# First mixers: scores of two neighbouring maps issued together, as products of 64 rows each

## The chip, the cores and the metric

One core of one Trainium2 chip runs the whole kernel. The metric is the device time of one execution in microseconds (us), taken as the median of several runs. A profiled execution beside them gives the trace that the rows below come from.

## What is computed

Two blocks of two layers each, on 256 tokens of width 1024, in float32. The first block is the one that matters here. Each of its two layers runs a feed-forward stage, a **mixer**, a second feed-forward stage and a gated embedding. The mixer is a windowed attention and a depthwise convolution side by side, gated and summed:

```python
u = rms_norm(h, norm_mix[i])
q, k, v, c, g = jnp.split(u @ w_in[i], splits, axis=-1)
q = rms_norm(q.reshape(B, S, N_HEADS, HEAD_DIM), q_norm[i])     # 8 heads of 64
k = rms_norm(k.reshape(B, S, KV_HEADS, HEAD_DIM), k_norm[i])    # 2 key heads of 64
y_attn = window_attention(q, k, v, sink[i], rel_bias) @ w_attn_out[i]
```

Four query heads share one key head. For every head the scores are 256 queries by 256 keys, each a sum over 64 products. The second block has mixers of its own (dilated, latent and differential attention), which the change leaves alone.

## The kernel before

**Matmuls and their weights.** Almost all the work is products of 256 rows with weights that stream in. The weights are cut into pieces (`ORDER`), mostly 1 MB. SyncE loads a piece into one of four `raw` slots; ScalarE rounds it to `whi` (line 1086, function `high`); VectorE forms the rest `wlo` (line 1608, function `low`); TensorE then makes three products for each of them (lines 498 to 500, 549 to 551, 576 and 582). ScalarE and VectorE prepare pieces that lie up to three ahead of the one TensorE works on (`AHEAD = 3`).

**Order of the work.** Every engine walks through the same program written out by hand. Side work, such as the attention of a mixer, is a Python generator on each engine, put into a list `bg`. A call of `tick()` advances every generator in the list by one step. TensorE ticks twice in a piece of four chunks (`rows`, lines 503 to 507), so that the attention's steps lie between runs of twelve products of 512 columns. VectorE ticks in `behind`: one tick, half of a piece of `wlo`, one tick, the other half. ScalarE ticks in `use`.

**The attention of a first mixer** (`attention1`, line 732 on TensorE, 1228 on ScalarE, 1849 on VectorE). Queries and keys are turned by products with the identity, so that the head dimension lies on the partitions. `qT` holds four pairs of query heads: in `qT[:, p, :]` the head that belongs to key head 0 lies on partitions 0 to 63 and the one of key head 1 on partitions 64 to 127. `kT` has two copies, `kT[:, s, :]`: copy s holds the keys of head s on its own 64 partitions, and zeros, written by VectorE (line 1910), on the other 64. The keys come out of the turn in one bank of PSUM, and ScalarE scales each half into its copy (line 1241). A product over all 128 partitions of `qT[:, p]` with `kT[:, s]` then gives the scores of one head.

There are eight maps (one per head), n = 0 to 7, pair p = n // 2 and key head s = n % 2. Step n of the generator does, on TensorE, `values1(n - 3)` (line 726), `turn1(n - 2)` (line 714) and `scores1(n)` (line 704). `scores1` makes two products, for queries 0 to 127 and 128 to 255, with 256 keys each. VectorE adds the bias and takes the row's extreme (line 1828), ScalarE takes the exponential (line 1218), and once TensorE has turned it (714), ScalarE copies it to `qn` (1226) as the stationary side of `values1`.

**Buffers for side work.** `spare()` (line 469) hands out three banks of PSUM in rotation, `P2` first half, `P2` second half, `SO` first half, and first waits for whatever frees the bank: for scores it is `s_mx` (VectorE has read both halves), for a turn it is `s_pTa` (ScalarE has copied it). The trace names these banks psP and psSO; the main products write psG.

**The same idea elsewhere in the kernel.** `scores2` (line 870), of the second block's mixers, handles maps of 32 and of 64 rows in pairs: it takes two banks, and issues for each half of the queries the product of the one map and then that of the other, on different partitions. Its first products have 128 columns (`SEGS`), the second ones 256. Maps of 96 rows are issued one at a time.

Of the kernel before, what the change touches and what calls it, by code (L numbers as in the profile page):

```python
# [8 lines left out]
F32 = mybir.dt.float32  # L9
F32R = mybir.dt.float32r  # L10
ACT = mybir.ActivationFunctionType
# [17 lines left out]
def piece(name, layer, chunks, *ranges):  # L29
    return (name, layer, tuple(chunks), tuple(ranges))  # L30
# [5 lines left out]
def halves(name, layer, *ranges, a=LO, b=HI):  # L36
    return [piece(name, layer, a, *ranges), piece(name, layer, b, *ranges)]
# [228 lines left out]
def build(nc, x_d, w_d, c_d, c2_d, rb_d, oh_d, msk_d, pt_d, line_d, out_d):  # L266
    with ExitStack() as ctx:
# [3 lines left out]
        def sem(name):  # L271
            return ctx.enter_context(nc.semaphore(name))
# [17 lines left out]
        def scope(n, names):  # L290
# [11 lines left out]
        M1 = scope(2, [  # L302
            ("y_hi", [128, 8, 256], F32R), ("y_lo", [128, 8, 256], F32R), ("thg", [128, 2, 2, 1024], F32),
            ("qs", [128, 2, 512], F32), ("qn", [128, 2, 512], F32), ("kv", [128, 2, 256], F32),
            ("qT", [128, 4, 256], F32), ("kT", [128, 2, 256], F32),
            ("acc", [128, 4, 256], F32), ("cpad", [128, 4 * 286], F32)])
        fill.close()
        c2 = sb("c2", [128, AT2["all"]])
# [10 lines left out]
        TB = (*BANKS["P2"], BANKS["SO"][0])  # L319
# [10 lines left out]
        s_xhi, s_xlo, s_tp, s_h, s_sq, s_ms, s_rs, s_half, s_dg, s_rsb, s_ones = (  # L330
            sem(n) for n in ("s_xhi", "s_xlo", "s_tp", "s_h", "s_sq", "s_ms", "s_rs", "s_half", "s_dg", "s_rsb", "s_ones"))
# [9 lines left out]
        s_lnc, s_nmu, s_lnq, s_lnv, s_lnr, s_ln, s_z, s_ychi, s_yclo = (  # L341
            sem(n) for n in ("s_lnc", "s_nmu", "s_lnq", "s_lnv", "s_lnr", "s_ln", "s_z", "s_ychi", "s_yclo"))

        s_qg, s_qs, s_qsq, s_qm, s_qr, s_qn, s_kv, s_km, s_kr, s_kn, s_kz, s_qT = (
            sem(n) for n in ("s_qg", "s_qs", "s_qsq", "s_qm", "s_qr", "s_qn", "s_kv", "s_km", "s_kr", "s_kn", "s_kz", "s_qT"))
        s_o, s_yhi, s_ylo, s_g, s_hm, s_cm, s_m = (sem(n) for n in ("s_o", "s_yhi", "s_ylo", "s_g", "s_hm", "s_cm", "s_m"))

        s_mx, s_ex, s_exs, s_pTa, s_pTv, s_pv = (
            sem(n) for n in ("s_mx", "s_ex", "s_exs", "s_pTa", "s_pTv", "s_pv"))
# [13 lines left out]
        def k(name, i=0, n=1):  # L363
            return cst[:, AT[name] + i:AT[name] + i + n]
# [7 lines left out]
        TBU = {}  # L372
# [7 lines left out]
        def flat(ap):  # L380
            return ap.rearrange("p a b -> p (a b)")
# [15 lines left out]
        thg, qs, qn, kv, qT, kT, acc = (M1[n] for n in ("thg", "qs", "qn", "kv", "qT", "kT", "acc"))  # L397
# [52 lines left out]
        def tensor(e):  # L450
# [18 lines left out]
            def spare(key):  # L469

                b = tb[1]
                TBU[key] = (tb[0], b)
                tb[0] += 1
                tb[1] = (b + 1) % 3
                f, i = spares[b]
                for s, v in f[i]:
                    e.wait_ge(s, v)
                return b

            def spare_frees(b, *when):  # L480
                f, i = spares[b]
                f[i] = list(when)
# [213 lines left out]
                free["SO"][1] = [(s_acc3, l + 1)]  # L696

            def scores1(l, n):
                p, s = n // 2, n % 2
                b = spare(("s1", l, n))  # L700
                e.wait_ge(s_qT, 4 * l + 4)
                e.wait_ge(s_kz, 2 * l + 2)
                for t in range(2):
                    i = e.matmul(TB[b][:, t * 256:t * 256 + 256], qT[:, p, t * 128:t * 128 + 128], kT[:, s, :], start=True, stop=True)
                i.then_inc(s_tp, 1)
                spare_frees(b, (s_mx, 2 * (8 * l + n) + 2))

            def turn1(l, n):
                b = spare(("p1", l, n))
# [8 lines left out]
            def values1(l, n):  # L718
                i4, s = n % 4, n % 2
                e.wait_ge(s_pTa, 8 * l + n + 1)  # L720
                for sm_, v in free["SO"][1]:
                    e.wait_ge(sm_, v)
                for t in range(2):
                    for kb_ in range(2):
                        c0 = kb_ * 256 + t * 128
                        i = e.matmul(O[:, t * 256 + i4 * 64:t * 256 + i4 * 64 + 64], qn[:, n % 2, c0:c0 + 128],
                                     kv[:, kb_, 128 + s * 64:192 + s * 64], start=kb_ == 0, stop=kb_ == 1)
                i.then_inc(s_pv, 1)
                if i4 == 3:
                    free["SO"][1] = [(s_o, 2 * (2 * l + n // 4) + 2)]  # L730

            def attention1(l):
                yield
                for n in range(2):
                    b = spare(("qT", l, n))
                    e.wait_ge(s_qn, 2 * l + 2)
                    for i in range(2):
                        for t in range(2):
                            ins = e.transpose(TB[b][:, i * 256 + t * 128:i * 256 + t * 128 + 128],
                                              qn[:, t, (2 * n + i) * 128:(2 * n + i) * 128 + 128], ident)  # L740
                    ins.then_inc(s_tp, 1)
                    spare_frees(b, (s_qT, 4 * l + n + 1))
                for _ in range(4):
                    yield
                b = spare(("kT", l))
                e.wait_ge(s_kn, 2 * l + 2)
                for t in range(2):
                    ins = e.transpose(TB[b][:, t * 128:t * 128 + 128], kv[:, t, 0:128], ident)
                ins.then_inc(s_tp, 1)
                spare_frees(b, (s_qT, 4 * l + 4))  # L750
                yield
                for n in range(11):
                    if n >= 3:
                        values1(l, n - 3)
                    if 2 <= n <= 9:
                        turn1(l, n - 2)
                    if n < 8:
                        scores1(l, n)
                    yield
                yield  # L760
                e.wait_ge(s_o, 4 * l + 4)
                for n in range(2):
                    transposes(("y", l, n), qs, (2 * n, 2 * n + 1), [(s_ylo, 2 * l + n + 1)])
# [294 lines left out]
        def scalar(e):  # L1058
# [169 lines left out]
            def attention1(l):  # L1228
                yield
                for n in range(2):  # L1230
                    u, b = TBU["qT", l, n]
                    e.wait_ge(s_tp, u + 1)
                    e.wait_ge(s_qg, l + 1)
                    e.activation(flat(qT[:, 2 * n:2 * n + 2, :]), TB[b][:, :], ACT.Copy, scale=sm[:, 0:1]).then_inc(s_qT, 1)
                for _ in range(4):
                    yield
                u, b = TBU["kT", l]
                e.wait_ge(s_tp, u + 1)
                for s in range(2):
                    r = slice(64 * s, 64 * s + 64)  # L1240
                    e.activation(kT[r, s, :], TB[b][r, 0:256], ACT.Copy, scale=k("k_norm", l)[r, :]).then_inc(s_qT, 1)
                yield
                for n in range(11):
                    if 2 <= n <= 9:
                        turn1(l, n - 2)
                    if n < 8:
                        softmax1(l, n)
                    yield
                yield
                for n in range(2):  # L1250
                    u, b = TBU["y", l, n]
                    e.wait_ge(s_tp, u + 1)
                    e.activation(flat(M1["y_hi"][:, 2 * n:2 * n + 2, :]), TB[b][:, :], ACT.Copy).then_inc(s_yhi, 1)
# [325 lines left out]
        def vector(e):  # L1579
# [236 lines left out]
            def scores1(l, n):  # L1816
                m = 8 * l + n
                hd = n // 2 + 4 * (n % 2)
                u, b = TBU["s1", l, n]
                for t in range(2):  # L1820
                    pb = tmp[:, (n % 4) * 512 + t * 256:(n % 4) * 512 + t * 256 + 256]
                    e.wait_ge(s_tp, u + 1)
                    if m == 0:
                        e.wait_ge(s_bias, 128)
                        e.wait_ge(s_dv, nsink_at)
                    if n >= 4:
                        e.wait_ge(s_tp, TBU["p1", l, n - 4][0] + 1)
                    e.tensor_tensor_reduce(pb, TB[b][:, t * 256:t * 256 + 256], bias[:, hd, 128 - 128 * t:384 - 128 * t], 1.0, nsink[:, 8 * l + hd:8 * l + hd + 1],
                                           ALU.add, ALU.min, sm[:, 64 + 2 * n + t:65 + 2 * n + t]).then_inc(s_mx, 1)
# [57 lines left out]
            def mixer1(l, nxt):  # L1887
# [17 lines left out]
                use(c0[0])  # L1905
                x_of_h("mix", l, 1)
                use(q[0])

                for s in range(2):
                    e.memset(kT[64 - 64 * s:128 - 64 * s, s, :], 0.0).then_inc(s_kz, 1)  # L1910
                e.memset(pad[:, :, 0:15], 0.0).then_inc(s_pad0, 1)
                e.memset(pad[:, :, 271:286], 0.0).then_inc(s_pad0, 1)
                e.tensor_scalar(sm[:, 0:1], k("q_norm", l), -0.125, None, ALU.mult, ALU.bypass).then_inc(s_qg, 1)
# [35 lines left out]
                for g in range(4):  # L1949
                    u = halves("w_in", l, (1792 + 512 * g, 2304 + 512 * g))  # L1950
# [36 lines left out]
                p, q = (piece("w_conv_out", l, LO, cols(g)) for g in range(2))  # L1987
# [8 lines left out]
                a, b = halves("w_o", l, cols(0)), halves("w_o", l, cols(1))  # L1996
# [530 lines left out]
```

## Time and profile before

| | |
|---|---|
| median of 3 runs | 1759.76 us (1759.19 to 1760.83) |
| the profiled execution's own time | 1759.31 us |
| its span, first to last instruction | 1757.5 us |
| TensorE busy | 1744.6 us, 99% of the span |
| VectorE busy | 1157.1 us, 66% |
| ScalarE busy | 930.6 us, 53% |
| read from memory | 300 MB, 171 GB/s over the span |

PE is TensorE's matmul and PEld its weight load, which overlaps it; DVE is VectorE, ACT ScalarE, POOL GpSimd, SP SyncE. Each float32 product with float32 operands shows as two MATMUL records, each with a LDWEIGHTS record of its own; the products with `whi` and `wlo` show as one. Matmuls are pipelined and their recorded ends are modelled, so durations of neighbours overlap; what a product costs is read from start to start.

### The profile page before, as it was taken

How to read it: one execution, taken by the hardware profiler on the slowest of the kernel's cores; microseconds unless marked ns; L12 is line 12 of the kernel's file. 1: busy time of each engine (PE TensorE's matmuls, PEld its weight loads, DVE VectorE, ACT ScalarE, POOL GpSimd, SP SyncE). 2: the span in 40 equal slices, each digit the busy share in tenths (PEclk: the TensorE clock that was granted, in tenths of full speed). 3: DMA queues.
4: the chain of work that ended last, by engine and by line, in shares of the span. 5: the costliest groups of instructions: out<-in, count | busy, mean ns of one | idle time of the engine just before them, and what ended most of it. 6: DMA issues, size and time to landing. Idle time of an engine off the chain costs nothing.

```text
span 1757.5 us, 26168 instructions
## 1 busy us (share of the span) xinstructions
PE 1744.6 (99%) x9886; PEld 1528.9 (87%) x9886; DVE 1157.1 (66%) x1700; ACT 930.6 (53%) x1376; POOL 26.5 (2%) x32
## 2 busy tenths in 40 slices
PE   9999999999999999999999999999999999999998
PEld 8888898898888988889889888889898888989886
DVE  6665588766655766568776665578575656857473
ACT  6554456655544555455655554467563546755352
POOL 0000000000000000000000000000000000000000
PEclk9999999999999999999999999999999999999999
DMA  8754523444545544552355445444265543435551
GB/s 314 219 192 169 214 102 139 175 176 183 192 170 190 210 183 173 190 198 101 128 190 189 183 173 192 163 157 163 99 213 192 192 165 112 152 120 194 202 181 48
DMA packets 45842, 303.04 MB, mean 172 GB/s; under 512 B 5104, under 2 KB 6256, under 8 KB 12312
## 3 DMA queue, kind: packets, MB, share of 16 engines
q1 hardware_dynamic: 45720, 301.36, 48.3%
q8 instruction: 83, 1.36, 0.3%
q14 instruction: 39, 0.32, 0.1%
HBM read 300.02 MB, written 1.31 MB: 171 GB/s over the span
## 4 chain that ended last, share of the span: by engine, by line
PE 97%; DVE 1%; ACT 1%; issue 1%; POOLq 0%; POOL 0%; ACTq 0%; DVEq 0%
PE psG L498 13%; PE psG L500 13%; PE psG L499 13%; PE psG L576 9%; PE psP L576 5%; PE psSO L576 5%; PE psG L582 5%; PE psG L549 3%; PE psG L550 3%; PE psG L551 3%; PE psSO L582 3%; PE psP L582 3%; PE psSO L693 2%; PE psP L615 1%; PE psSO L906 1%; PE psSO L500 1%
## 5 line engine op out<-in xcount | busy, mean ns | idle before, releaser
L1608 DVE TENSOR_TENSOR wlo<-raw,whi 128x1024 fp32r<-128x1024 f32 (+4 forms) x388 | 656.3, 1704 | 312.0 <-ACT whi L1086 311.8
L1086 ACT ACTIVATE whi<-raw 128x1024 fp32r<-128x1024 f32 (+4 forms) x388 | 554.1, 1444 | 276.3 <-PE psG L500 162.1
L498 PE MATMUL psG<-whi,x 128*128 128x512 f32 (+3 forms) x544 | 210.6, 387 | 0.0
L500 PE MATMUL psG<-whi,x 128*128 128x512 f32 (+3 forms) x544 | 200.9, 369 | 0.0
L499 PE MATMUL psG<-wlo,x 128*128 128x512 f32 (+3 forms) x544 | 200.5, 369 | 0.0
L498 PE MATMUL psG<-whi,hid_hi 128*128 128x512 f32 x472 | 184.1, 390 | 0.0
L500 PE MATMUL psG<-whi,hid_lo 128*128 128x512 f32 x472 | 183.6, 389 | 0.0
L499 PE MATMUL psG<-wlo,hid_hi 128*128 128x512 f32 x472 | 183.6, 389 | 0.0
L576 PE MATMUL psG<-x,whi 128*128 128x512 f32 x704 | 179.8, 392 | 0.0
L549 PE MATMUL psG<-x,wlo 128*128 128x256 f32 x512 | 147.5, 288 | 1.4 <-DVE wlo L1608 1.4
L576 PEld LDWEIGHTS psG<-x,whi 128*128 128x128 f32 x704 | 126.6, 189 | 22.6
L550 PE MATMUL psG<-x,whi 128*128 128x256 f32 x512 | 144.8, 283 | 0.0
L551 PE MATMUL psG<-x,whi 128*128 128x256 f32 x512 | 144.8, 283 | 0.0
L576 PE MATMUL psP<-x,whi 128*128 128x512 f32 x416 | 130.1, 394 | 0.0
L576 PE MATMUL psSO<-x,whi 128*128 128x512 f32 x416 | 128.9, 391 | 0.0
L498 PEld LDWEIGHTS psG<-whi,x 128*128 128x128 f32 x544 | 102.4, 188 | 16.1 <-issue 2.0
L500 PEld LDWEIGHTS psG<-whi,x 128*128 128x128 f32 x544 | 102.2, 188 | 15.6
L499 PEld LDWEIGHTS psG<-wlo,x 128*128 128x128 f32 x544 | 102.5, 188 | 14.1
L500 PEld LDWEIGHTS psG<-whi,hid_lo 128*128 128x128 f32 x472 | 88.6, 188 | 18.5
L499 PEld LDWEIGHTS psG<-wlo,hid_hi 128*128 128x128 f32 x472 | 88.6, 188 | 18.3
L498 PEld LDWEIGHTS psG<-whi,hid_hi 128*128 128x128 f32 x472 | 88.6, 188 | 18.1
L582 PEld LDWEIGHTS psG<-x,wlo 128*128 128x128 f32 x704 | 96.0, 190 | 6.8
(382 smaller groups left out, 2773.0 us busy)
## 6 DMA issues: line engine op xcount, KB each, us to landing
raw<-in_w SPq DMA_DIRECT2D x261, 1024.0 KB, 4.8
raw<-in_w SPq DMA_DIRECT2D x12, 768.0 KB, 4.2
raw<-in_w SPq DMA_DIRECT2D x14, 512.0 KB, 3.3
raw<-in_w SPq DMA_DIRECT2D x4, 576.0 KB, 3.8
raw<-in_w SPq DMA_DIRECT2D x4, 432.0 KB, 3.2
bias<-line_scratch SPq DMA_DIRECT2D x8, 192.0 KB, 10.3
h<-in_x SPq DMA_DIRECT2D x2, 512.0 KB, 5.9
out<-h SPq DMA_DIRECT2D x2, 512.0 KB, 2.7
```

Source lines behind the costliest of these rows:

```text
L498: e.matmul(o, ph, wh, start=first, stop=False)
L499: e.matmul(o, ph, wl, start=False, stop=False)
L500: i = e.matmul(o, pl, wh, start=False, stop=last)
L549: e.matmul(o, wl, x_hi[:, c, :], start=first and n == 0 and m % 2 == 0, stop=False)
L550: e.matmul(o, wh, x_lo[:, c, :], start=False, stop=False)
L551: i = e.matmul(o, wh, x_hi[:, c, :], start=False, stop=last and n == len(spec[2]) - 1 and m % 2 == 1)
L576: i = e.matmul(BANKS[bks[m // 2]][m % 2], wh, x[:, c, :], start=first and n == 0, stop=end)
L582: i = e.matmul(BANKS[bks[m // 2]][m % 2][:, 256:512], wl, x_hi[:, c, :], start=False, stop=False)
L615: ins = e.transpose(o, src[:, t, c * 128:c * 128 + 128], ident)
L693: e.matmul(O[:, 0:256], diag[:, tap % 16, :], pad[:, 1, tap:tap + 256], start=tap == 0, stop=tap == TAPS - 1).then_inc(s_cv, 1)
L1086: e.activation(w_at(whi, j, off, n), raw[:, j % RAW, off:off + n], ACT.Copy).then_inc(s_hi, count)
L1608: e.tensor_tensor(w_at(wlo, j, off, n), raw[:, j % RAW, off:off + n], f32(w_at(whi, j, off, n)), ALU.subtract).then_inc(s_lo, count)
```

## The change

The second copy of the keys goes: `kT` becomes 128 by 256, written by one ScalarE instruction over all partitions, and the zeros and their semaphore `s_kz` go. On TensorE, `scores1` does nothing for odd n; for even n it takes two banks and issues four products of 64 rows, in the order (queries 0 to 127: map n, map n + 1), (queries 128 to 255: map n, map n + 1). The last product of each map signals. VectorE waits, for either map, for the signal of the odd one.

```diff
-            ("qT", [128, 4, 256], F32), ("kT", [128, 2, 256], F32),
+            ("qT", [128, 4, 256], F32), ("kT", [128, 256], F32),
...
             def scores1(l, n):
-                p, s = n // 2, n % 2
-                b = spare(("s1", l, n))
-                e.wait_ge(s_qT, 4 * l + 4)
-                e.wait_ge(s_kz, 2 * l + 2)
-                for t in range(2):
-                    i = e.matmul(TB[b][:, t * 256:t * 256 + 256], qT[:, p, t * 128:t * 128 + 128], kT[:, s, :], start=True, stop=True)
-                i.then_inc(s_tp, 1)
-                spare_frees(b, (s_mx, 2 * (8 * l + n) + 2))
+
+                if n % 2:
+                    return
+                bs = [spare(("s1", l, n + s)) for s in range(2)]
+                e.wait_ge(s_qT, 3 * l + 3)
+                for t in range(2):
+                    for s, b in enumerate(bs):
+                        r = slice(64 * s, 64 * s + 64)
+                        i = e.matmul(TB[b][:, t * 256:t * 256 + 256], qT[r, n // 2, t * 128:t * 128 + 128], kT[r, :], start=True, stop=True)
+                        if t == 1:
+                            i.then_inc(s_tp, 1)
+                for s, b in enumerate(bs):
+                    spare_frees(b, (s_mx, 2 * (8 * l + n + s) + 2))
...
-                for s in range(2):
-                    r = slice(64 * s, 64 * s + 64)
-                    e.activation(kT[r, s, :], TB[b][r, 0:256], ACT.Copy, scale=k("k_norm", l)[r, :]).then_inc(s_qT, 1)
+                e.activation(kT[:, :], TB[b][:, 0:256], ACT.Copy, scale=k("k_norm", l)).then_inc(s_qT, 1)
...
             def scores1(l, n):
                 m = 8 * l + n
                 hd = n // 2 + 4 * (n % 2)
-                u, b = TBU["s1", l, n]
+                b = TBU["s1", l, n][1]
+
+                u = TBU["s1", l, n | 1][0]
...
-
-                for s in range(2):
-                    e.memset(kT[64 - 64 * s:128 - 64 * s, s, :], 0.0).then_inc(s_kz, 1)
```

The values that wait for `s_qT` change with it, from four signals a layer to three.

## Rows read from the trace of the kernel before

**Rows 1.** The page: busy time by engine, and TensorE's granted clock in 40 slices.

```profile
PE 1744.6 (99%) x9886; PEld 1528.9 (87%) x9886; DVE 1157.1 (66%) x1700; ACT 930.6 (53%) x1376; POOL 26.5 (2%) x32
...
PEclk9999999999999999999999999999999999999999
```

**Rows 2.** All waits of TensorE (six lines; first two, last): total us, times, longest.

```profile
PE psG L549 <- DVE wlo L1608: 1.4, 1, 1.4
PE psSO L1042 <- POOL ones L2369: 1.0, 1, 1.0
...
PE psSO L906 <- DVE mix L2096: 0.5, 2, 0.2
```

**Rows 3.** The tile kT: instructions that touch it, ns min/median/max, first and last start.

```profile
L704 PE MATMUL psP<-kT,qT x40: 377/379/382, 264.0 to 854.1; 128*128 128x256 f32 x40
...
L704 PE MATMUL psSO<-kT,qT x24: 377/379/382, 260.3 to 859.0; 128*128 128x256 f32 x24
L1910 DVE MEMSET kT<- x4: 272/272/272, 208.8 to 775.0; 64x256 f32 x4
L1241 ACT ACTIVATE kT<-psP,cst x4: 471/472/473, 257.8 to 824.2; 64x256 f32<-64x256 f32 x4
```

**Rows 4.** Timeline of TensorE, a step with scores, then one without (start, us, ...).

```profile
272.48 0.61 PE L714 MATMUL psP<-cst,tmp 128*128 128x128 f32 x4
...
274.02 0.40 PE L499 MATMUL psG<-wlo,x 128*128 128x512 f32 x1
...
296.88 0.61 PE L714 MATMUL psP<-cst,tmp 128*128 128x128 f32 x4
...
297.56 0.40 PE L499 MATMUL psG<-wlo,x 128*128 128x512 f32 x1
```

**Rows 5.** Timeline of TensorE, second block: a pair of 64-row maps, then no scores.

```profile
1233.01 0.50 PE L891 MATMUL psP<-cst,tmp 128*128 128x128 f32 x3
1233.44 0.37 PE L880 MATMUL psP<-qkcT,qkc 64*128 64x128 f32 x1
1233.45 0.37 PE L880 MATMUL psSO<-qkcT,qkc 64*128 64x128 f32 x1
1233.65 0.27 PE L880 MATMUL psP<-qkcT,qkc 64*128 64x128 f32 x1
...
1233.77 0.38 PE L880 MATMUL psP<-qkcT,qkc 64*128 64x256 f32 x1
...
1233.98 0.38 PE L880 MATMUL psP<-qkcT,qkc 64*128 64x256 f32 x1
...
1234.30 0.50 PE L498 MATMUL psG<-whi,c_hi 128*128 128x512 f32 x1
1234.63 0.39 PE L499 MATMUL psG<-wlo,c_hi 128*128 128x512 f32 x1
...
1236.39 0.50 PE L891 MATMUL psP<-cst,tmp 128*128 128x128 f32 x3
...
1236.96 0.39 PE L499 MATMUL psG<-wlo,c_hi 128*128 128x512 f32 x1
```

**Rows 6.** Timeline of VectorE in layer 0, around the first two maps.

```profile
261.40 0.48 DVE L1828 CUSTOM_DVE_ANT_0 tmp<-psSO,bias,sm 128x256 f32<-128x256 f32 x1
...
262.21 1.67 DVE L1788 SCALAR_TENSOR_TENSOR acc<-cpad,cst,acc 128x256 f32<-128x256 f32 x4
263.80 1.22 DVE L1608 TENSOR_TENSOR wlo<-raw,whi 128x1024 fp32r<-128x1024 f32 x1
265.03 0.48 DVE L1828 CUSTOM_DVE_ANT_0 tmp<-psP,bias,sm 128x256 f32<-128x256 f32 x1
```

**Rows 7.** Timeline of TensorE: the scores of maps 0 and 2.

```profile
260.34 1.02 PE L704 MATMUL psSO<-kT,qT 128*128 128x256 f32 x4
...
268.04 1.03 PE L704 MATMUL psSO<-kT,qT 128*128 128x256 f32 x4
```

**Rows 8.** Busy time by engine over the maps of layer 0.

```profile
258.00:296.00 38.00, 38.00 (x203) 32.79 (x203) 32.21 (x82) 26.02 (x62) 0.00 (x0) 1.00 0.32 112
```

More of the change, by code:

```diff
@@ L342, in build @@
             sem(n) for n in ("s_lnc", "s_nmu", "s_lnq", "s_lnv", "s_lnr", "s_ln", "s_z", "s_ychi", "s_yclo"))
-        s_qg, s_qs, s_qsq, s_qm, s_qr, s_qn, s_kv, s_km, s_kr, s_kn, s_kz, s_qT = (
-            sem(n) for n in ("s_qg", "s_qs", "s_qsq", "s_qm", "s_qr", "s_qn", "s_kv", "s_km", "s_kr", "s_kn", "s_kz", "s_qT"))
+        s_qg, s_qs, s_qsq, s_qm, s_qr, s_qn, s_kv, s_km, s_kr, s_kn, s_qT = (
+            sem(n) for n in ("s_qg", "s_qs", "s_qsq", "s_qm", "s_qr", "s_qn", "s_kv", "s_km", "s_kr", "s_kn", "s_qT"))
         s_o, s_yhi, s_ylo, s_g, s_hm, s_cm, s_m = (sem(n) for n in ("s_o", "s_yhi", "s_ylo", "s_g", "s_hm", "s_cm", "s_m"))
@@ L741, in attention1 @@
                     ins.then_inc(s_tp, 1)
-                    spare_frees(b, (s_qT, 4 * l + n + 1))
+                    spare_frees(b, (s_qT, 3 * l + n + 1))
                 for _ in range(4):
@@ L749, in attention1 @@
                 ins.then_inc(s_tp, 1)
-                spare_frees(b, (s_qT, 4 * l + 4))
+                spare_frees(b, (s_qT, 3 * l + 3))
                 yield
```

## The prediction

> **What bounds the kernel now.** I read the page first: TensorE is busy 99% of the span and its granted clock stands in the top tenth in all 40 slices, the 2.4 GHz level [rows 1]. Then the list of TensorE's waits: it has six lines, the longest single wait is 1.4 us at the start, and no line names the first mixers' score, turn or value products (lines 704, 714, 726) [rows 2]. Then the stretch of layer 0 in which the eight maps are made: TensorE 38.0 of 38.0 us busy, VectorE 32.2, ScalarE 26.0, DMA a share of 0.32 [rows 8]. So TensorE's issue order is the critical path there, and a microsecond taken from it comes off the end, as long as nothing new makes it wait. The last views are timelines of TensorE, read from start to start.
>
> **What the scores cost now.** The tile's view has 40 + 24 = 64 records of line 704 [rows 3]: 2 layers x 8 maps x 2 products x 2 records, each of 256 columns on 128 rows. The cost of one map is the difference of two steps that are otherwise alike. From the first turn record to the first product of line 499 behind the step it takes 274.02 - 272.48 = 1.54 us with scores and 297.56 - 296.88 = 0.68 without [rows 4]: 0.86 us for a map, that is four records of about 0.216 each, and 1.73 for a pair of maps. All 16 maps are alike within 0.01 us. Sum now: 8 x 1.73 = 13.8 us.
>
> **What a pair will cost.** The second block has exactly such pairs: records of psP and psSO that start 0.01 us apart and go on together [rows 5], so two halves of the rows do work at the same time. By the same difference: 1234.63 - 1233.01 = 1.62 us with the pair, 1236.96 - 1236.39 = 0.57 without, so 1.05 us for it. But there the first of the two query halves has 128 columns; here both have 256. Two records of each map grow by what 128 columns more cost. The third record starts 0.11 behind the second (128 columns) and the fourth 0.21 to 0.22 behind the third (256 columns), so each grows by 0.107. The open point is the first record: it lasts 0.37 where the second of equal width lasts 0.27, and the second starts 0.21 behind it, not 0.11. Either the 0.1 is added to the streaming (weights are loaded with nothing to hide them, then the columns run), and a first record of 256 columns takes 0.32; or it is a floor that 256 columns would fill anyway. The other edge of the pair speaks for adding: the 512-column product behind it lasts 0.50 where others last 0.39, and its successor starts 0.33 later where 0.23 is usual. There 512 columns, far over any such floor, did not hide it. I take adding: 1.05 + 2 x 0.107 = 1.27 us for a pair, with 1.05 + 0.107 = 1.16 as the other value.
>
> **Sum.** A pair saves 1.73 - 1.27 = 0.46 us (0.57 by the floor). Two layers of four pairs: 8 x 0.46 = 3.7 us. The bounds of a pair: at best no cost at its edges, four steps of 0.22 = 0.88, a saving of 0.85, in all 6.8 us; at worst no overlap at all, priced below.
>
> What the edges cost is the point. In the pair of the trace the first record starts 0.09 late, loads for 0.1 unhidden, the product behind starts 0.09 late and loads 0.11 unhidden: 0.39 us of the 0.85 that the overlap brings is given back [rows 5]. The Trainium skill, TensorEngine Tiling (Array Packing), section Key Properties, speaks against the change here: changing the tiling mode drains TensorE. The trace agrees, with these 0.39 us; the page names no price, and without the drain the sum would be the 6.8 us of the upper bound.
>
> **The rest of the change.** *Zeros and their wait.* The four memsets are 0.27 us each on VectorE [rows 3] and lie over 50 us ahead of the first scores; VectorE is 5.8 us short of busy in the 38 us of [rows 8], so nothing waited for them and nothing is gained. If that cover were gone they would be worth 0.5 us a layer. *One key copy.* Two ScalarE instructions of 0.47 us in a row from 257.8 become one of 128 rows; the copies were ready by 258.8 and the scores start at 260.3 [rows 3, 7]. Zero, hidden by 1.5 us of main products. *Signals.* One per map before and after. *Order on VectorE.* For an even map it now waits for the whole pair, about 0.3 us longer after its start than for one map, and then finds the odd one ready. No DMA is added or moved, and SyncE's and GpSimd's queues are the same.
>
> *The wait that is added.* With two banks taken at once, the rotation changes. The order of banks becomes: turn n - 2, map n, map n + 1, turn n - 1, turn n, map n + 2, map n + 3. So map n + 2 takes the bank of map n + 1 and waits for VectorE to have read it (`s_mx`), where it used to take a turn's bank. Queued behind it on TensorE is everything, the main products of line 498 first. When is it due? For n = 0 the pair starts at 260.34. Map 2 was at 268.04 [rows 7]; with map 1's 0.86 gone and the pair 0.41 longer than one map (1.27 - 0.86) it is asked for at about 267.6. VectorE needs: pair done at about 261.6, evaluation of map 0 0.8, four taps 1.6, a part of `wlo` 1.2, evaluation of map 1 0.9 [rows 6]: 266.1. It is in time by 1.5 us. For later pairs two steps with values and turns lie between: from map 3's turn at 272.48 back to map 2 at 268.04 is already 4.4 us for less than one step, so two take over 8.8 and the margin is over 3 us. The other takers (turns) wait for what they or the values just before them waited for already. Zero.
>
> So the profiled execution goes from 1759.31 to 1755.6 and the median, which lies 0.45 above it, from 1759.76 to **1756.1 us**, a gain of 0.21%. About 0.2% (3.5 us) is what a measurement of this kernel can tell from no change, so the forecast sits on that line.
>
> **The rivals.**
> *A. The first load is a floor.* 8 x 0.57 = 4.5 us, 1755.2. For it: nothing but that no first record of 256 columns is in the trace. Against it: the exit of the pair.
> *B. Loads don't overlap within a row group.* If every record of 64 rows had to wait for its own weights, three more loads of 0.107 would be exposed in a pair: 1.27 + 0.32 = 1.59, a saving of 0.14, in all 1.1 us, 1758.7. Against it: the third record starts 0.11 behind the second and the fourth 0.22 behind the third, which leaves no room for a load [rows 5]. The Trainium skill, TensorE: Matmul & The Clock Gate, Part 3 (The mechanism), says that weight loads overlap running products only when the row group differs, and successive records of one map here do share theirs. By that rule rival B would be the result; the trace shows it for the first record of a pair only.
> *C. The halves run one after the other.* Eight records of 0.215 and the edges' 0.39: 2.1 us a pair against 1.73, 3.0 us slower, 1762.8 (still within 0.2%). Against it: the second block's pairs, which run at once.
> *D. Slower: the wait for VectorE's reading of map n + 1 becomes real.* Its place is the bank of map n + 2, its point a delay of VectorE by 1.5 us in the first pair and over 3 in the others. If VectorE came a whole step later (4.9 us: 3.5 for map 2, about 1.5 for maps 4 and 6), TensorE would stand 6.5 us a layer, 13 in all: 13 - 3.7 = 9 us slower, 1769. For it: VectorE is 85% busy there. Against it: nothing makes it a step late, since it begins with map 0 at 261.40, 0.04 us after the scores end (260.34 + 1.02), and so was waiting for them [rows 6, 7].
> *E. Part of it is given back* by main products that run up against VectorE or ScalarE: a saving of 1 to 3 us, 1757 to 1758.7. Against it: TensorE has no wait for `wlo` but the one at the start [rows 2].
>
> **How the numbers follow.** Forecast (saving 3.2 to 4.1) 0.62, A 0.15, B 0.05, C 0.04, D 0.05, E 0.09. Faster by over 0.2% is all of A and a little over half of the forecast: 0.15 + 0.34 = 0.49. Slower by over 0.2% is D and the far end of C: 0.06. Within 0.2%: 0.45. The range goes from A with 0.3 us for the medians' own scatter, 1754.9, to most of E and a part of B, 1758.2.
>
> **What would show it.** In the trace after: 64 records of line 704's successor on 64 rows, in twos 0.01 us apart; a pair step 1.27 us longer than one without scores, its second record 0.32 behind the first (0.21 under A), the later ones 0.22 apart (0.32 under B); odd steps without scores; no wait of TensorE for line 1828's successor (D). Span down by 3.7, all of it between 258 and 296 us and its twin in layer 1. Steps of 1.5 or more for eight records of a pair, or new lines in TensorE's waits, would prove me wrong.

## The result and the profile after

The changed kernel takes **1755.9 us** (median of 13 runs, 1755.3 to 1756.4) against 1759.3 before (13 runs, 1758.8 to 1760.8): 3.4 us less. The ratio is 0.998 with a 95% interval of 0.9972 to 0.9988, so it is faster, by 0.2%. A second set beside later experiments gave 1755.75 against 1759.31. The forecast was 1756.1, in a range of 1754.9 to 1758.2, and a gain of 3.7 us from a base of 1759.76 (three runs).

The busy times of the page, to be held against [rows 1]:

```profile
span 1754.1 us, 26154 instructions
...
PE 1741.5 (99%) x9886; PEld 1522.6 (87%) x9886; DVE 1154.8 (66%) x1696; ACT 928.2 (53%) x1374; POOL 26.5 (2%) x32
```

TensorE has as many records as before, 9886, and is busy 3.1 us less; that it is still at 99% says only that it is still the bound. The tile kT, against [rows 3]: the 64 records are there, now on 64 rows; VectorE's four memsets are gone and one copy on 128 rows stands where two on 64 were.

```profile
L707 PE MATMUL psP<-kT,qT x40: 376/376/480, 260.7 to 851.5; 64*128 64x256 f32 x40
...
L707 PE MATMUL psSO<-kT,qT x24: 376/376/480, 260.7 to 842.1; 64*128 64x256 f32 x24
L1244 ACT ACTIVATE kT<-psP,cst x2: 477/477/477, 258.1 to 822.2; 128x256 f32<-128x256 f32 x2
```

The timeline of TensorE through one burst, the third pair of layer 0, and then a step with its scores left out, against [rows 4]:

```profile
276.71 0.61 PE L719 MATMUL psSO<-cst,tmp 128*128 128x128 f32 x4
277.25 1.13 PE L707 MATMUL psP<-kT,qT 64*128 64x256 f32 x8
278.31 0.50 PE L498 MATMUL psG<-whi,x 128*128 128x512 f32 x1
278.64 0.39 PE L499 MATMUL psG<-wlo,x 128*128 128x512 f32 x1
...
281.18 1.00 PE L731 MATMUL psSO<-kv,qn 128*128 128x64 f32 x8
282.01 0.61 PE L719 MATMUL psSO<-cst,tmp 128*128 128x128 f32 x4
...
282.69 0.40 PE L499 MATMUL psG<-wlo,x 128*128 128x512 f32 x1
```

From the first turn record (L719) to the product of L499 behind: 278.64 - 276.71 = 1.93 us with the pair, 282.69 - 282.01 = 0.68 without. A pair costs 1.25 us here (1.25 to 1.26 before rounding, over the eight bursts) where two single maps cost 1.73. The next burst, whose banks are psP and psSO so that each record stands alone, shows from what:

```profile
286.61 0.48 PE L707 MATMUL psP<-kT,qT 64*128 64x256 f32 x1
286.61 0.48 PE L707 MATMUL psSO<-kT,qT 64*128 64x256 f32 x1
286.93 0.38 PE L707 MATMUL psP<-kT,qT 64*128 64x256 f32 x1
286.93 0.38 PE L707 MATMUL psSO<-kT,qT 64*128 64x256 f32 x1
287.14 0.38 PE L707 MATMUL psP<-kT,qT 64*128 64x256 f32 x1
287.15 0.38 PE L707 MATMUL psSO<-kT,qT 64*128 64x256 f32 x1
287.36 0.38 PE L707 MATMUL psP<-kT,qT 64*128 64x256 f32 x1
287.36 0.38 PE L707 MATMUL psSO<-kT,qT 64*128 64x256 f32 x1
```

Two records start together each time. The second two come 0.32 behind the first, the others 0.21. The first lasts 0.48 where the rest last 0.38: its 0.1 is added to its columns, not hidden in them.

**Where the time went** is read by following the same product through both traces. Four products of TensorE before:

```profile
9.76 0.38 PE L549 MATMUL psG<-x,wlo 128*128 128x256 f32 x1 [1.42 <-DVE wlo L1608]
...
293.54 0.40 PE L499 MATMUL psG<-wlo,x 128*128 128x512 f32 x1
...
859.43 0.40 PE L499 MATMUL psG<-wlo,x 128*128 128x512 f32 x1
...
1749.94 0.39 PE L525 MATMUL psG<-wlo,hid_hi 128*128 128x512 f32 x1
```

and the same four after:

```profile
10.03 0.39 PE L549 MATMUL psG<-x,wlo 128*128 128x256 f32 x1 [1.42 <-DVE wlo L1611]
...
292.05 0.40 PE L499 MATMUL psG<-wlo,x 128*128 128x512 f32 x1
...
856.20 0.40 PE L499 MATMUL psG<-wlo,x 128*128 128x512 f32 x1
...
1746.54 0.39 PE L525 MATMUL psG<-wlo,hid_hi 128*128 128x512 f32 x1
```

The changed kernel is 0.27 us late at its first main product, which lies ahead of everything that changed (this offset differs from one profiled execution to the next by some tenths); 1.49 early behind layer 0's last scores; 3.23 early behind layer 1's; 3.40 early at the end. So layer 0's maps gave 1.76 us and layer 1's 1.74, 3.5 together, and all of it came through. The last 0.17 us, between the third landmark and the end, stand far behind the maps, at 1240 us, and -0.27 + 3.50 + 0.17 is the 3.40 of the end. TensorE's list of waits has the same six lines as the list before, none of them new. The one there (line 498, for VectorE's `c_lo`) fell from 0.9 to 0.7 us; it is 0.9 in two other kernels that have the pairs, so these 0.17 us are not a gain of the change that can be counted on.

### The profile page after: what moved, and what is told of

Read it like the earlier page. It is cut to its first block, busy times and chain, and to the rows that moved or that the text cites. A ratio compares the mean times of both kernels' runs of the same rounds, so it can differ in the third digit from the quotient of the medians.

```text
span 1754.1 us, 26154 instructions
## 1 busy us (share of the span) xinstructions
PE 1741.5 (99%) x9886; PEld 1522.6 (87%) x9886; DVE 1154.8 (66%) x1696; ACT 928.2 (53%) x1374; POOL 26.5 (2%) x32
## 4 chain that ended last, share of the span: by engine, by line
PE 97%; DVE 1%; ACT 1%; issue 1%; POOLq 0%; POOL 0%; ACTq 0%; DVEq 0%
PE psG L498 14%; PE psG L500 13%; PE psG L499 13%; PE psG L576 9%; PE psP L576 5%; PE psSO L576 5%; PE psG L582 5%; PE psG L549 3%; PE psG L550 3%; PE psG L551 3%; PE psSO L582 3%; PE psP L582 3%; PE psSO L693 2%; PE psP L615 1%; PE psSO L911 1%; PE psSO L499 1%
## 5 line engine op out<-in xcount | busy, mean ns | idle before, releaser
L499 PE MATMUL psG<-wlo,x 128*128 128x512 f32 (+3 forms) x544 | 200.4, 368 | 0.0
L499 PE MATMUL psG<-wlo,hid_hi 128*128 128x512 f32 x472 | 183.6, 389 | 0.0
L499 PEld LDWEIGHTS psG<-wlo,x 128*128 128x128 f32 x544 | 102.5, 188 | 13.9
L499 PEld LDWEIGHTS psG<-wlo,hid_hi 128*128 128x128 f32 x472 | 88.6, 188 | 18.3
```

The costliest lines, as they stand in the source:

```text
L499: e.matmul(o, ph, wl, start=False, stop=False)
```

## Experiments

Each kernel starts from the changed one; "changed kernel" is 1755.9 us. Each time is a median with runs of the kernel before on the same chip, which gave 1759.2 to 1759.4.

### One map at a time, on 64 rows

```diff
-                if n % 2:
-                    return
-                bs = [spare(("s1", l, n + s)) for s in range(2)]
+                s, b = n % 2, spare(("s1", l, n))
+                r = slice(64 * s, 64 * s + 64)
...
                 for t in range(2):
-                    for s, b in enumerate(bs):
-                        r = slice(64 * s, 64 * s + 64)
-                        i = e.matmul(...)
+                    i = e.matmul(...)
+                i.then_inc(s_tp, 1)
```

> The changed kernel with the maps issued one at a time again, each on its own 64 rows. Edge theory (going from 128-row to 64-row products and back costs 0.4 us each time, whether or not two halves work at once): a map costs 0.86 + 0.40 = 1.26 us, 16 of them 20.2 us against 13.8 before, so 6.3 us over before, about 1765.7 us, and 1602 - 342 = 1260 ns per map in the timeline. Rival (the edges come from alternating between the halves, 64 rows alone are free): 0.86 us a map as before, 1759.3 us.

Measured: 1765.8 us (ratio to before 1.0036, 1.0023 to 1.0049). In its timeline a map's step takes 1.25 us more than a step without scores, where 128 rows take 0.86. A map issued alone on half the rows is a loss of 0.4 us; the gain is in two at once, and the 0.4 is the price of the excursion, paired or not.

### The pair's products in another order

```diff
-                for t in range(2):
-                    for s, b in enumerate(bs):
+                for s, b in enumerate(bs):
+                    for t in range(2):
                         r = slice(64 * s, 64 * s + 64)
```

> The changed kernel with the pair's four products in another order: both query halves of map n, then both of map n + 1. In-order theory: only the last record of the one map and the first of the other can overlap, so a pair is some seven steps of 0.216 us plus the edges' 0.40: 1.9 us, 0.2 over before and 0.65 over the changed kernel, in all about 1760.8 us. Rival (the engine's queue finds the free half by itself): 1.26 us a pair, 1755.9 us.

Measured: 1756.15 us (ratio 0.998, 0.9971 to 0.999): the rival, not my expectation. The timeline of TensorE shows how. The program has four records on psSO and behind them four on psP, but they start in pairs all the same, 0.01 us apart:

```profile
260.94 0.48 PE L707 MATMUL psSO<-kT,qT 64*128 64x256 f32 x1
260.96 0.48 PE L707 MATMUL psP<-kT,qT 64*128 64x256 f32 x1
261.26 0.38 PE L707 MATMUL psSO<-kT,qT 64*128 64x256 f32 x1
261.28 0.38 PE L707 MATMUL psP<-kT,qT 64*128 64x256 f32 x1
```

The program built for TensorE from this kernel does hold them in the written order, all records of the one map and then all of the other, so it was not rearranged ahead of the chip. TensorE starts a product for the idle half past products that wait for the busy one. (The changed kernel shows it on a small scale: each float32 product is two records, so its order is two of the one map, two of the other, and they too start one and one.) The order written in the change is not what makes the halves overlap; that both maps are queued together is.

### The order of the change, with 128 rows

```diff
-            ("qT", [128, 4, 256], F32), ("kT", [128, 256], F32),
+            ("qT", [128, 4, 256], F32), ("kT", [128, 2, 256], F32),
...
-                        i = e.matmul(..., qT[r, n // 2, t * 128:t * 128 + 128], kT[r, :], start=True, stop=True)
+                        i = e.matmul(..., qT[:, n // 2, t * 128:t * 128 + 128], kT[:, s, :], start=True, stop=True)
```

with zeros, copies and semaphore as before the change.

> The order of the change alone: two banks at once, both maps of a pair issued together, the odd step empty, VectorE waiting for the odd map; but the keys in two copies with zeros and products over 128 rows as before. Row theory (the gain is the two halves working at once): 1.73 us a pair and the time of before, 1759.3 us, within 0.3. Rival (part of the gain is the order: fewer interruptions of the main stream, a wait that goes): a time between, 1757 to 1758.5.

Measured: 1759.95 us (ratio 1.0002, 0.9993 to 1.0012): no gain. The median lies 0.6 us over the one expected, more than the 0.3 allowed; its interval holds no change, and in the layers only 0.2 is lost. The eight records now follow one another:

```profile
278.09 0.61 PE L720 MATMUL psSO<-cst,tmp 128*128 128x128 f32 x4
278.53 1.89 PE L708 MATMUL psP<-kT,qT 128*128 128x256 f32 x8
...
280.49 0.40 PE L499 MATMUL psG<-wlo,x 128*128 128x512 f32 x1
```

280.49 - 278.09 - 0.68 = 1.72 us, two single maps. By the same four landmarks as above its layers lose 0.09 and 0.13 us against before. So the order alone gains nothing.

### Every product twice

```diff
-                for t in range(2):
+                for t in (0, 0, 1, 1):
                     for s, b in enumerate(bs):
```

with the signal left on each map's last product.

> The changed kernel with every score product issued twice in a row (the same result written again), so sixteen records in a pair's burst. Edge theory (0.40 us once per burst): four more steps of 0.216, 0.86 us a pair, 6.9 us over the changed kernel, 1762.8 us. Rival (the 0.40 belongs to every set of products): 1.26 us more a pair, 10.1 us, 1766.0. With loads that don't overlap within a half (rival B) each step would be 0.32: 10.2 us as well, and the timeline would show it.

Measured: 1762.8 us (ratio 1.0018, 1.0009 to 1.0027), 6.9 over the changed kernel, as the edge theory has it. The extra records come at the usual step:

```profile
260.36 0.38 PE L707 MATMUL psSO<-kT,qT 64*128 64x256 f32 x1
260.37 0.38 PE L707 MATMUL psP<-kT,qT 64*128 64x256 f32 x1
260.58 0.38 PE L707 MATMUL psSO<-kT,qT 64*128 64x256 f32 x1
260.58 0.38 PE L707 MATMUL psP<-kT,qT 64*128 64x256 f32 x1
260.80 0.38 PE L707 MATMUL psSO<-kT,qT 64*128 64x256 f32 x1
```

0.22 from one to the next, which is what 256 columns take by themselves (128 columns take 0.11 [rows 5]), with room for no load: rival B falls, and the 0.4 us are paid once per burst.

### The keys as before, the products paired

`kT` in two copies with zeros, as in the experiment with 128 rows, but products on 64 rows of `kT[r, s, :]`.

> The changed kernel's paired products, but the keys as before: two copies with zeros, two ScalarE instructions, four memsets and their semaphore. My theory (these lay under other work): the time of the changed kernel within 0.3 us, and PE's stretch of the maps unchanged. Rival (the shorter key chain or VectorE's 0.65 us a layer were worth something): up to 1 us slower than the changed kernel.

Measured: 1756.0 us (ratio 0.9982, 0.9973 to 0.999). Its layers gain 1.78 and 1.74 us by the landmarks. Memsets and the second copy were free, as the prediction priced them.

### VectorE late for map 1, a little and a lot

```diff
                 u = TBU["s1", l, n | 1][0]
+                if n == 1:
+                    for q in range(2):
+                        e.wait_ge(s_dv, step(e.memset(M1["idle"][:, :], 0.0)))
```

on a tile of its own, 128 by 512; the second kernel has seven where this has two.

> The changed kernel with two memsets of 512 columns on VectorE ahead of its evaluation of map 1, about 1.3 us in each layer. In the changed kernel's trace map 1's second half is read by 266.3 and TensorE asks for the bank at 267.9, a margin of 1.5 us. Margin theory: no change (within 0.3 us), no wait of TensorE. Rival (VectorE is the bound there in some other way, through wlo or the taps): up to 2.6 us slower.

Measured: 1756.2 us (ratio 0.9981, 0.9972 to 0.999), no new wait.

> The same with seven memsets, about 4.5 to 5 us in each layer. Margin theory: TensorE waits 3 to 3.5 us for VectorE at the scores of map 2 in each layer, shown as a wait of the score products for the evaluation line, and the time is 6 to 7 us over the changed kernel, 1762 to 1763; the later pairs have recovered. If the wait is not at the bank but elsewhere (wlo, the convolution's end), the list of waits names another line.

Measured: 1764.4 us (ratio 1.0028, 1.0017 to 1.0038), 8.5 over the changed kernel, more than expected. TensorE's waits, both at the predicted place:

```profile
PE psP L707 <- DVE sm L1836: 3.1, 1, 3.1
PE psSO L707 <- DVE sm L1836: 3.1, 1, 3.1
PE psG L549 <- DVE wlo L1611: 1.4, 1, 1.4
```

The rest stands behind the waits. The timeline of TensorE, then its busy times in the 4 us (last columns: granted clock, DMA share, GB/s):

```profile
267.27 0.60 PE L719 MATMUL psP<-cst,tmp 128*128 128x128 f32 x4
270.99 0.45 PE L707 MATMUL psSO<-kT,qT 64*128 64x256 f32 x1 [3.11 <-DVE sm L1836]
...
272.55 0.63 PE L499 MATMUL psG<-wlo,x 128*128 128x512 f32 x1
272.97 0.63 PE L500 MATMUL psG<-whi,x 128*128 128x512 f32 x1
273.40 0.63 PE L498 MATMUL psG<-whi,x 128*128 128x512 f32 x1
```

```profile
271.50:275.50 4.00, 4.00 (x14) 2.94 (x12) 4.00 (x11) 4.00 (x11) 0.00 (x0) 0.58 0.16 33
```

Products that come 0.23 us apart elsewhere come 0.43 apart, and the granted clock of the stretch is 0.58: most of it runs at 1.2 GHz. Before it fell TensorE had stood still for 3.1 us, having run without a wait since 10 us. Behind the wait in layer 1 it is the same: 0.54 granted from 841 to 846 us.

The waits and these views are of the profiled execution, one of the two slowest of the eight (1766.2 us, 10.3 over the changed kernel). By the landmarks its layers lose 4.7 and 5.8 us against the changed kernel: 3.1 of waiting in each, and 1.6 and 2.7 of slow products behind. The eight runs lie between 1763.3 and 1766.2 us, with a mean granted clock of 0.998 or 0.999 in the four fastest and 0.996 in the two slowest, where the changed kernel has 0.999. So a wait of this length costs itself and then, here, one to three microseconds more, and that part differs from one execution to the next. If the waits were 3.1 us in the median run too, which no trace shows, it lost (8.5 - 6.2) / 2, some 1.2 us, behind each.

### The first four maps in one burst

If the edges are paid per burst, a burst of four maps saves one. A fourth bank is free at that point: `SO`'s second half, which `values1` uses from step 3 on.

```diff
-        TB = (*BANKS["P2"], BANKS["SO"][0])
+        TB = (*BANKS["P2"], *BANKS["SO"])
...
-                if n % 2:
+                if n % 2 or n == 2:
                     return
...
+                ns = range(4) if n == 0 else (n, n + 1)
+                if n == 0:
+                    for s_, v in free["SO"][1]:
+                        e.wait_ge(s_, v)
+                    TBU["s1", l, 0] = (tb[0], 3)
+                    tb[0] += 1
+                    free["SO"][1] = [(s_mx, 16 * l + 2)]
+                bs = {m: 3 if m == 0 else spare(("s1", l, m)) for m in ns}
```

> The changed kernel with the first four maps in one burst (map 0 in the bank of the values, maps 1 to 3 in the three spare ones): one burst of 64-row products less in each layer. Edge theory: 0.40 us a layer less, 0.8 us in all, 1755.1 us, four pairs of records 0.216 apart between the two pairs with no gap. Rival (a new wait for the banks, or VectorE's later evaluations of maps 2 and 3, takes it back): the time of the changed kernel or more.

Measured: 1754.9 us (8 runs, 1754.7 to 1755.6; ratio to before 0.9975, 0.9965 to 0.9986). The timeline of TensorE has sixteen records in 1.9 us, and the burst costs 2.13 us where two pairs cost 2.52. Of these 0.39 us a layer keeps 0.34: by the landmarks its two layers gain 2.10 and 2.09 us, the changed kernel's 1.76 and 1.74. That is 0.7 us in all, against 0.8 expected.

```profile
260.37 1.14 PE L715 MATMUL psSO<-kT,qT 64*128 64x256 f32 x8
261.34 1.03 PE L715 MATMUL psP<-kT,qT 64*128 64x256 f32 x8
262.30 0.51 PE L498 MATMUL psG<-whi,x 128*128 128x512 f32 x1
```

Then both kernels once more, side by side:

> The changed kernel again, on the same chip as the next run and with its runs of before, so that the two can be compared: 1755.9 us within 0.3.

> The kernel of e8_four again beside the changed kernel: 0.8 to 1.0 us under it, about 1755.0 us. If the difference between them is under 0.4 us, the saving of one burst a layer is not shown by times, only by the timeline.

Measured: 1755.75 us (0.9979, 0.997 to 0.9988) and 1755.1 us (0.9976, 0.9966 to 0.9986). The four-map kernel has the lower median in both sets, by 1.0 and by 0.6 us, and its spans are 1753.0 and 1752.9 us against 1754.1 twice. The 0.6 of the second set, the one with both on one chip, is under the 0.8 to 1.0 expected and over the 0.4 that the expectation asked for. 15 of the four-map kernel's 16 runs lie below the changed kernel's median of their set, but the intervals of the two ratios overlap. So the saving is shown by the timeline and has the medians with it; its size is not measured by the times.

## Why the prediction was right, point by point

*The bound.* TensorE's issue order was the critical path in the stretch of the maps, and what was taken from it came off the end: 3.5 us there, 3.4 in the medians. The time came out closer than the gain, and that is luck: the base of three runs (1759.76) lay 0.4 us over the median of thirteen (1759.33), and a forecast of 3.7 less from the better base is 1755.6, off by 0.3 us, where 1756.1 is off by 0.2.

*What two maps cost now.* 1.73 us; the kernel with 128 rows in the new order has 1.72. That this was streaming and not interruption is shown by it too.

*What a pair costs.* Forecast 1.27 us, measured 1.26. The choice that mattered was between a first load that is added and one that is a floor, 1.27 against 1.16. It was read from the exit of a pair of the second block [rows 5], where 512 columns had not hidden a load. The first record of 256 columns now lasts 0.48 and the next starts 0.32 behind it: it is added, and A falls. That pairs elsewhere in the same kernel existed, with their edges, is why the sum came out at 3.7 and not at the 6.8 of overlap alone.

*The edges.* 0.4 us for each excursion into 64 rows, shown three ways: paid 16 times with single maps (6.5 us over before), not paid again when the burst is doubled, and saved twice by the burst of four maps (0.39 us of the burst each time). This agrees with the rule of the Trainium skill, TensorEngine Tiling (Array Packing), Key Properties, that the prediction weighed (changing the tiling mode drains TensorE); its cost here is 0.4 us where the page has no figure.

*Rival B and its rule.* Steps of 0.22 in the doubled burst leave no room for a load within a row group. The line of the Trainium skill, TensorE: Matmul & The Clock Gate, Part 3 (The mechanism), that the prediction cited (loads overlap running products only when the row group differs) doesn't hold here. The same section also has a load for the background weight buffer pulled ahead, which the prediction left out, and with that the steps of 0.22 agree. Only the first record of a burst, which has no product of its half ahead of it, shows its load.

*Zeros, copy, signals.* Priced at nothing, and the kernel that has them back is 0.1 us from the changed one in its median.

*The added wait.* Its margin was put at 1.5 us for map 2: 1.3 us of memsets used none of TensorE's time, some 4.6 us made it wait 3.1 in each layer, which puts the margin at 1.5. For the later pairs it was put at over 3 us; in the trace after, map 3 is read by 273.5 us and the next pair starts at 277.25, over 3.5 us. One step of the reasoning was wrong without changing this: map 2 does not take map 1's bank in the first pair, nor did it take a turn's before. Maps 0 and 2 are both on psSO, before [rows 7] and after. It is map 3 that takes map 1's bank, and since both banks are taken ahead of the first product, TensorE waits for VectorE's reading of map 1 all the same. Nor had VectorE time in hand at map 0: in the trace before, a part of `wlo` of 1.22 us starts at 260.15, right ahead of the evaluation at 261.40. Rival D's price of a VectorE late in every pair was not tested, since the experiment delays it once in each layer and the later pairs show no wait; what it did show is that the price left out the clock.

*What the sum missed.* By the bursts alone the layers should give 8 x 0.468 = 3.7 us; they give 3.5. The missing 0.2 lies in the main products between the bursts. Behind the scores of a step with values, the run up to the next step took 281.40 - 278.90 = 2.50 us before and takes 281.18 - 278.64 = 2.54 now, and as much behind an odd step. The kernel with the new order and 128 rows loses the same 0.2, so half rows are not needed for it. The new order is not needed either: with one map at a time on 64 rows, in the order of before, the same run takes 2.54 us too. Why a run is 0.03 to 0.04 us longer in all these kernels than behind the steps of before is open. It was not tested further.

*The odds.* I had the change faster by over 0.2% with 0.49 and within 0.2% with 0.45. The measured 3.4 us is 0.2%, on the line between the two, and its interval holds both. The prediction took 0.2% for what can be told from no change; the interval is 0.08% to either side, so a gain half as large would still have been clear.

## What to carry to other kernels

Two products on separate 64-row halves run at once, but count the edges: entering and leaving cost 0.4 us here, nearly half of what a pair's overlap brings, and a map alone on half the rows is a pure loss. So put as many of them into one burst as there are free banks; the one burst of four maps tried here gave 0.34 us more in each layer. When a trick is already used elsewhere in the kernel, read its whole excursion there, from the last product before to the second one behind, rather than the overlapped part.

## What the runs showed of the hardware

- TensorE does not keep the program's order between halves: with both products of one map queued ahead of the other map's, records of the two still started 0.01 us apart. The Trainium skill, TensorE: Matmul & The Clock Gate, Part 3 (The mechanism), states that matmuls start strictly in program order; the timeline of this experiment shows otherwise, and the measurement decides.
- Each of two standstills of TensorE of 3.1 us, one in each layer and in stretches otherwise without gaps, was followed by products at the 1.2 GHz level: 0.58 granted over 4 us behind the first, products of 512 columns 0.43 apart instead of 0.23. In the profiled execution this cost 1.6 and 2.7 us on top of the waits.
